# Rotary halves exchanged by four SBUF to SBUF transfers from ScalarE's queue, in place of a permutation matmul

## The reference

```python
def rope(x, pos):
    ...
    x1, x2 = x[..., : d // 2], x[..., d // 2:]
    return jnp.concatenate([x1 * cos - x2 * sin, x2 * cos + x1 * sin], axis=-1)

def diff_branch(q, k, v, g, ...):
    q = rope(q, pos) * (DIFF_HD ** -0.5)      # 4 heads, 2 parts of 64 channels each
    k = rope(k, pos)
    ...
        s = jnp.einsum('cbhqd,cbhkd->cbhqk', qblk, k)
        p = jax.nn.softmax(s, axis=-1)
        w = p[0] - lam * p[1]
        return jnp.einsum('bhqk,bhkv->bhqv', w, v)
```

## Time and profile before

| | |
|---|---|
| median of 3 runs | 4258.22 us (4257.85 to 4259.90) |
| profiled execution: its span | 4251.8 us |
| profiled execution: its own time | not given beside the span; the median of the runs lies 6.4 us above the span |
| first block, to about 2341 us of the span | 2341 us |
| layer 0 of the second block, about 2341 to 3320 us | 979 us |
| layer 1, about 3320 us to the end | 931 us |
| busy: TensorE, VectorE, ScalarE, GpSimd | 89%, 45%, 34%, 23% of the span |

### The profile page before, as it was taken

How to read it: one execution, slowest core, us unless ns; L and a number is a source line. 1 busy time by engine, 2 the same in 40 slices (tenths; PEclk the granted TensorE clock), 3 DMA queues, 4 the chain that set the end, 5 groups by cost and what they waited for, 6 DMA issues and landing times.

```text
span 4251.8 us, 75982 instructions
## 1 busy us (share of the span) xinstructions
PE 3767.7 (89%) x33819; PEld 2325.2 (55%) x34140; DVE 1895.1 (45%) x2057; ACT 1463.4 (34%) x1839; POOL 991.7 (23%) x438
## 2 busy tenths in 40 slices
PE   6989999999999999998999878988889888988887
PEld 3556666666666665446544445555554455555554
DVE  3456454655555554341323344254542254254542
ACT  4222223232332312231213243344553243344552
POOL 2423223332423332131152201111102210111002
PEclk9999999999999999999999988989999988989999
DMA  2111111111111113333320200100002100100002
GB/s 97 51 37 51 37 46 50 47 51 41 56 42 51 50 57 115 118 133 114 118 86 30 97 17 11 40 21 21 31 25 101 41 17 11 40 21 25 26 28 87
DMA packets 61623, 227.55 MB, mean 54 GB/s; under 512 B 6832, under 2 KB 8560, under 8 KB 60784
## 3 DMA queue, kind: packets, MB, share of 16 engines
q1 hardware_dynamic: 52224, 189.64, 13.2%
q10 hardware_dynamic: 9072, 33.03, 1.9%
HBM read 174.93 MB, written 47.71 MB: 52 GB/s over the span
## 4 chain that ended last, share of the span: by engine, by line
PE 74%; DVE 13%; ACT 7%; issue 3%; POOL 2%; DMA 2%; ACTq 0%; DVEq 0%; SPq 0%; POOLq 0%
PE psum L1009 72%; DVE arena L2141 5%; ACT arena L1596 4%; DVE arena L2144 4%; PE psum L1012 2%; DVE arena L2612 2%; ACT wh L1596 1%; DMA arena<-in_w_proj_conv 1%; POOL arena L2671 1%; POOL hl L2671 1%; POOL wl L2671 1%; ACT arena L2075 0%; DVE arena L2521 0%; DVE arena L2148 0%; DVE arena L2546 0%
## 5 line engine op out<-in xcount | busy, mean ns | idle before, releaser
L1009 PE MATMUL psum<-arena 64*64 64x32 f32 (+11 forms) x23468 | 1398.7, 257 | 278.9 <-ACT arena L1596 128.1
L1009 PEld LDWEIGHTS psum<-arena 64*64 64x64 f32 (+6 forms) x23468 | 999.7, 142 | 703.4 <-issue 410.0
L2671 POOL TENSOR_TENSOR wl<-arena,wh 128x1024 bf16<-128x1024 f32 (+1 forms) x203 | 491.7, 2422 | 2208.3 <-ACT wh L1596 2205.3
L1009 PE MATMUL psum<-hh,wh 128*128 128x512 f32 x3248 | 914.0, 425 | 67.1 <-ACT hh L1596 23.5
L1596 ACT ACTIVATE arena<-psum 128x512 f32<-128x512 f32 (+4 forms) x660 | 416.2, 631 | 1124.9 <-PE psum L1009 836.6
L1009 PE MATMUL psum<-hh,wl 128*128 128x512 bf16 (+1 forms) x3028 | 773.7, 393 | 24.4 <-issue 9.1
L1009 PE MATMUL psum<-hl,wh 128*128 128x512 bf16 x3147 | 757.8, 384 | 21.2 <-issue 10.7
L1009 PEld LDWEIGHTS psum<-hh,wh 128*128 128x128 f32 x3248 | 614.8, 195 | 263.4 <-issue 49.8
L2141 DVE TENSOR_TENSOR arena<-psum,arena 128x512 f32<-128x512 f32 (+3 forms) x472 | 299.8, 635 | 928.2 <-PE psum L1009 594.3
L2144 DVE SCALAR_TENSOR_TENSOR arena<-arena 128x1024 f32<-128x1024 f32 x356 | 584.5, 1642 | 168.0 <-ACT arena L1596 151.3
L2671 POOL TENSOR_TENSOR arena<-arena 128x1024 f32<-128x1024 f32 (+4 forms) x142 | 365.6, 2575 | 877.0 <-ACT arena L1596 474.9
(11 more groups left out here) (38 smaller groups left out, 781.8 us busy)
## 6 DMA issues: line engine op xcount, KB each, us to landing
arena<-in_w_in SPq DMA_DIRECT2D x161, 512.0 KB, 3.6
scr_g<-arena ACTq DMA_DIRECT2D x24, 512.0 KB, 2.6
arena<-scr_g SPq DMA_DIRECT2D x24, 512.0 KB, 4.4
arena<-in_w_out SPq DMA_DIRECT2D x24, 512.0 KB, 3.6
arena<-in_w_mem_kv SPq DMA_DIRECT2D x16, 512.0 KB, 3.6
scr_x<-arena SPq DMA_DIRECT2D x16, 512.0 KB, 3.6
arena<-scr_x SPq DMA_DIRECT2D x16, 512.0 KB, 6.8
arena<-in_x SPq DMA_DIRECT2D x8, 512.0 KB, 10.8
```

The source lines that it names most:

```text
L1009: return pe.e.matmul(o, l, r, start=start, stop=stop)
L2671: return pool.seq.tensor_tensor(o, a, b, op)
```

## The change

The matmul step `rope` and its pair of banks go. After its copy, ScalarE waits for the copy's own completion and issues four transfers of 32 partitions by 1024 columns (128 KB each) from `PX` to a new buffer `SWAP`, each 32-partition group going to the place of its neighbour. VectorE's `turned` waits for the four to land, multiplies `SWAP` by `sin` in place, and only then waits for GpSimd's product before it adds. GpSimd's product, whose step had the name `rope`, now has the name `turned`, and so stands in GpSimd's program where `turned` stands in the list.

```diff
+    SWAP = sl(5120, 1024)
...
             yield 0.25
-            held(("rope", L, h, i), ("rope", L, h, i))
             yield 0.25
             do("turned", L, h, i)
-            ps.leave(("rope", L, h, i))
...
-        def rope(L, h, i):
-            use = ("rope", L, h, i)
-            pe.wait_ge(*at("dq_copy", L, h, i))
-            sums(use, "rope", perm, PX)
...
             ps.give(p, ("dq_copy", L, h, i))
+            act.wait_ge(*act.own)
+            for j in range(4):
+                a, b = slice(32 * j, 32 * j + 32), slice(32 * (j ^ 1), 32 * (j ^ 1) + 32)
+                act.e.dma_start(SWAP[a], PX[b]).then_inc(*(act.land("swapped", L, h, i) if j == 3 else act.land("swapped", L, h, i, j)))
...
         def turned(L, h, i):
-            use = ("rope", L, h, i)
-            dve.wait_ge(*at("rope", *use))
+            dve.wait_ge(*at("swapped", L, h, i))
             dve.wait_ge(*at("consts2"))
+            tt(SWAP, SWAP, sin, MUL).then_inc(*dve.up("rope_sin", L, h, i))
+            x = QK[h % 2][i]
             dve.wait_ge(*at("rope_cos", L, h, i))
-            tt(PX, pair(use), sin, MUL).then_inc(*dve.up("rope_sin", L, h, i))
-            ps.give(use, ("rope_sin", L, h, i))
-            x = QK[h % 2][i]
-            tt(x, x, PX, ADD).then_inc(*dve.up("rope_add", L, h, i))
+            tt(x, x, SWAP, ADD).then_inc(*dve.up("rope_add", L, h, i))
...
-        def rope(L, h, i):
+        def turned(L, h, i):
             pool.wait_ge(*at("dq_copy", L, h, i))
```

More of the change, by code:

```diff
@@ L951, in build @@
                      " so_copy so_sum so_rs so_norm sg_sig sg_out"),
-            ("diff", "dv_copy dv_turn dq_copy rope turned qk dmax dexp dr e1 dw dt WT dv do do_sq do_sum do_rs do_norm dg_sig dg_out")):
+            ("diff", "dv_copy dv_turn dq_copy turned qk dmax dexp dr e1 dw dt WT dv do do_sq do_sum do_rs do_norm dg_sig dg_out")):
         for name in names.split():
@@ L1509, in tensor_program @@
                     matt=matt, sv_turn=sv_turn, ga_up=ga_up, diag=diag, lev=lev, kt=kt, st=st, so=so, so_sum=so_sum,
-                    dv_turn=dv_turn, rope=rope, qk=qk_, dt=dt, dv=dv, do_sum=do_sum)
+                    dv_turn=dv_turn, qk=qk_, dt=dt, dv=dv, do_sum=do_sum)
         for name, *a in plan:
@@ L2786, in pool_program @@
         does = dict(init=init, load=load, split=split, cs=cs, kh=kh, bk=bk, eye=eye, decay=decay, prep=prep, sx=sx, sxe=sxe, gnorm=gnorm, gaff=gaff, merge=merge,
-                    usil=usil, qf=qf, rope=rope, resid=resid)
+                    usil=usil, qf=qf, turned=turned, resid=resid)
         for name, *a in plan:
```

## The result

The changed kernel takes 4279.1 us, median of 4 runs (4274.6 to 4288.9), beside 4259.1 us for the kernel before on the same chip: ratio 1.0048, interval 1.0035 to 1.0061. It is slower by 20 us, where the forecast was 23 us faster. The profiled run took 4274.6 us, span 4272.7.

A forecast was written before the change was run, and what follows sets the result against it. TensorE was taken to hold three quarters of the chain, often waiting on ScalarE. Places A to H summed to -11.3 us a layer, doubled to -22.6 from 4258.2, giving 4236 us; range 4221 to 4262.

The forecast's parts named there:

- The likeliest case: Whole kernel: the places sum to -11.3 us a layer, -22.6 in all, giving 4236 us.
- F: GpSimd's product comes behind its `hz` weights load, delaying block 4's scores, with low clock after: +3.6 us, bounds +1.8 and +6.5.
- G: `dv` waits for `WT`, now behind ScalarE's issues, and not for `rope`: +0.2 us a layer.
- C: `WT` and `e1` come 1.9 us later with room; VectorE's 0.68 us wait on TensorE goes: -0.7, bounds -2 and +0.5.
- E: Around `so_sum`: TensorE saves 1.7 us, ScalarE comes 1.9 later but had waited 1.15: 0, between -1 and +1.
- X: Time from the end of `dq_copy` to the fourth transfer's landing: 3.9 us, bounds 3.6 and 10.5.
- A: TensorE goes on with the projection at once, without the removed matmuls: -1.3 us a layer.
- D: `dv`, `st` and `kt` no longer held behind `rope`'s 6.86 us wait; head 1's scores start earlier: -8.0 us.
- B: Scores' start unchanged, but `ga` gets a long-free bank pair and loses its 2.17 us wait: -2.0 us.
- the first rival: Slower: the four transfers do not overlap, landing 10.5 us after the copy; +9.7 a layer, 4277.6 us; chance 0.15.
- H: Four matmuls removed between busy neighbours, -1.7, and `hz` gets another bank pair, -1.4: together -3.1 us.
- The second rival: No change: local gains given back through bank shifts and ScalarE's added work; -3.2 a layer, 4251.8, or nothing; chance 0.2.

The follow-up runs named there:

- x9: Changed kernel with seven or eight long-met waits in TensorE's queue where each permutation stood, restoring later instruction numbers; 1.0006 of the kernel before.
- x5: Changed kernel with eight empty instructions in TensorE's queue at each of the 16 places where the permutation stood; 1.0032 of the kernel before.
- x13: Changed kernel, transfers of heads 0 to 2 issued from the sine table, unread and not waited for, TensorE's numbers kept by met waits; 4255.6 us, 0.9983.
- x10: Changed kernel without the transfers and their issues (rotation left out), TensorE's numbers kept by met waits; 0.9950 of the kernel before.
- x14: Changed kernel with GpSimd's product at its old queue place and TensorE's numbers kept by met waits; 4256.4 us, 0.9994 of the kernel before.
- x11: Kernel before, with transfers only at A and B (issued by SyncE) and D and H (by ScalarE), plus met waits; 4232.7 us, 0.9932.
- x12: Kernel before, no transfers, TensorE's permutation step at D moved behind `dv` and `st` in both layers; 4251.6 us, 0.9973.
- x1: Changed kernel with GpSimd's product back at its old queue place, ahead of the weights' remainder; 4275.2 us.

## Why the prediction was wrong

The likeliest case (-22.6) failed, in three steps.

**The removal of 16 steps from TensorE's program was counted as time saved alone.** "Removed on TensorE: 16 steps ... some 1.7 us each" left out that everything behind them moves up in the program. That cost 11 to 18 us (x9 against the changed kernel and x5) of a miss of 43, at stretches that the forecast did not look at. TensorE's timeline of the kernel before has such waits, so that they exist could have been seen, not where they would go:

```profile
2493.41 0.50 PE L1009 MATMUL psum<-arena 32*32 32x32 f32 x34 [2.83 <-issue]
...
2550.71 0.69 PE L1009 MATMUL psum<-arena 32*32 32x32 f32 x40 [2.44 <-issue]
...
3047.57 0.27 PE L1009 MATMUL psum<-arena 64*32 64x32 f32 x10 [1.65 <-issue]
```

**"About 1.9 us, 16 times, in front of whatever ScalarE does next" was too small and its place too lightly taken.** Four issues took 2.45 us at most places, 2.89 at F and 3.44 at G. C, E and G were put at -0.7, 0 and +0.2; with kept numbers they are -0.2, +0.8 and +3.8, without transfers -0.5, -3.3 and -1.2. The issues of all 16 places are 14 us, with head 3's landings (x13 against x10).

**"X ... I take 3.9" was too small everywhere, and far too small beside loads.** E and A had 4.2 and 4.6, D and G 5.2, but B 7.0 and F 9.5; the landings of 12 places cost 10 us (x9 against x13). The bound 10.5 was meant for transfers that wait for each other; it was reached at F (x14) beside weight loads from the other queue. The Trainium skill's rule (DMA: Bandwidth & Descriptors, Rules for kernel authors), that transfers to disjoint halves of the partitions serialize, spoke for the first rival. The traces do not agree for these quarters: the four land 4.2 us after the copy at E, and at B when SyncE issues them, less than four times the 2.1 us of the earlier trace rows. x11's trace has the landing of each quarter, here of the 16 that SyncE issued:

```profile
L2883 SPq DMA_DIRECT2D arena<-arena x16: 507/592/600, 2406.9 to 3379.6; - x16
...
DMA to landing us min/median/max: 2.2/2.3/2.7
```

At B they are issued and land some 0.63 us apart, and each takes 2.3, so none waits for the one before to land. So the rival's time, 4277.6, came near to what was measured for a reason that was true at one place a layer.

What held: H to 0.3 us; D to 2 us (-6.0 for -8.0), and the cause, TensorE's order (x12); the bank at B, though the late landing took the gain of A and B back (without transfers they give -3.1, forecast -3.3); at F GpSimd's queue (3 us a layer in the traces of x1 and the changed kernel, 1.2 and 2.6 in those of x14 and x9) and the longer stretch at 1.2 GHz, so that F measured +6.7 against +3.6 and its bound of +6.5. And the removal itself: with kept numbers and no transfers 21 us were gained (x10). The second rival, gains given back, named banks and ScalarE; banks did the opposite.

With positions kept, the sum is: removal -21, issues (with head 3's landings) +14, the other landings +10, together +3 (x9). GpSimd's place at F is in all three runs and costs some 5 (x14 against x9, with intervals that overlap).

Three readings of the prediction do not bear what they carry. The layers are not alike: with kept numbers and no transfers layer 0 gained 9.9 us and layer 1 17.1, so doubling layer 0 was not safe. The earlier trace rows show that eight loads were issued in 4.16 us, not that they moved at once. And 4262 is not half-way to the slow case: half-way from 4258.2 to 4277.6 is 4267.9, which the result also lies above.

## What to carry to other kernels

Before a change that adds or removes instructions on a busy engine is judged by its time, compare its long waits for nothing (short ones can be missing records), and repeat the run with the instruction numbers restored; here that was worth 11 to 18 us, and the exchange at all 16 places, once repaired, nothing that could be told. Transfers put where an engine has just finished a step on the critical path cost their issue time there, and land late beside loads from another queue: use them only at places with slack (A, B, D, H gave 0.7%, of which D's order alone gives 0.3% by x12), and from the queue whose loads would otherwise run beside them. Look first whether moving the blocking step in its engine's order gives the gain without any new work.

## What the runs showed of the hardware that was not expected

TensorE can run out of instructions. The page counts 268 transfers of kind instruction in q8, 4.39 MB: 16 KB each, and 4.39 MB over 34,076 weight loads and as many matmuls is 64 bytes an instruction, so 256 to a transfer. In the wait of 4.11 us before 3068.48 such a transfer begins at 3066.01 and takes 1.13 us, and TensorE goes on 1.35 us after its end. So it is at every wait of this kind over 1.2 us: in the 17 traces there are 135, and each ends 1.2 to 1.6 us after the end of an instruction transfer, where a moment taken at random in the changed kernel's second block would lie so with a chance of 2%. They also lie at one place of the program: in the eight traces with every record, all 49 end within two neighbouring instructions of the same place in a block of 256 (number 193 or 194, counted from 0 at the first instruction in the trace). That is why a shift of eight instructions moves them. Not every block has such a wait. A group of 128 short matmuls, 256 instructions, runs in 1.29 us, about as long as one transfer takes; that this is why the waits lie in such groups is argued, not shown.

An exchange issued from ScalarE's queue beside 512 KB loads of SyncE's landed after 7.0 (B) and 9.5 us (F); issued by SyncE ahead of those loads, after 4.2 and 5.4. Single issues on ScalarE took from 0.51 to 2.18 us.
